# First gate block: four of the eight mixes of the normed rows made by GpSimd in place of VectorE

## The chip, the cores and the metric

The kernel runs on one core of a Trainium2 chip. The metric is the device time of one execution in microseconds (us); lower is better. The kernel before has a median of 2643.79 us over three runs (2643.77 to 2644.37).

## The reference

One layer of an encoder trunk over 512 rows of width 2048, in float32. With h the RMS-normed input:

```python
proj = jnp.einsum('bsd,de->bse', h, w_in[l])
(u_pool, c_b, c_c, c_x, q, k, v, qi, ki, wi, gate_logits) = jnp.split(proj, pts, axis=-1)
...
g = jax.nn.sigmoid(gate_logits).reshape(B, S, N_BRANCH, D)
merged = (g[:, :, 0] * (a @ w_pool_out) + g[:, :, 1] * (bconv @ w_conv_out) + g[:, :, 2] * (c @ w_attn_out))
x = x + merged @ w_o
x = x + square(relu(rmsnorm(x) @ w_ff1)) @ w_ff2
```

The change lies in the product of h with the gate columns of `w_in` (3 x 2048 columns), in the first of its six blocks of 1024 columns.

## The kernel before

**Arithmetic.** TensorE multiplies in a short format, so each operand is split into a rounded part ("hi", a copy by ScalarE) and a rest ("lo", source minus hi, by VectorE), and each product is made of three matmuls: hi with hi, hi with lo, lo with hi. The large products (gates, output projection, MLP) go further: each block of the product is made by a scheme of seven block products in place of eight (numbers n = 0 to 6). For that, quarters of both operands are first added to and subtracted from each other. These sums are the "mixes".

**A gate block** J (0 to 5) is 28 pieces: one for each of the seven products n and each of four groups g of weight rows. The lists `order_of(J)` set the order. For block 0 the order is: (0,g) and (5,g) in turn for g = 0 to 3 (pieces 0 to 7), (1,g) (8 to 11), (4,g) (12 to 15), (3,g) and (2,g) in turn (16 to 23), (6,g) (24 to 27). For each piece ScalarE copies the weight block to `g_wh` (`hi2`, L1473), VectorE makes `g_wl` (`lo2`, L2161), and TensorE runs twelve 128x512 matmuls (L1182 to L1184, function `granule`). The weights have four slots, so the copy of piece k waits until TensorE is done with piece k - 4. The weight blocks land over SyncE's DMA queue.

**The rows' side in block 0.** The normed rows come back from DRAM into `xin` (`h_block`), in two halves h. Products 1, 4, 2 and 3 need mixed quarters. For each (n, h) there are three steps: the mix in `xin` (`mix_gs`), the rounded copy by ScalarE (`hi_gs`, L1598, into `gs` or `act_hi`), and the rest by VectorE (`lo_gs`, L2332, into `gs` or `act_lo`). Their order is

```python
GS_SPLITS = ((1, 0), (1, 1), (4, 0), (4, 1), (2, 0), (3, 0), (2, 1), (3, 1))
```

The semaphores `gs_mixed`, `gs_hi` and `gs_lo` count the three steps. Mix (2,h) overwrites the quarter that mix (1,h) made, so it waits for the rest of (1,h). Mix (3,h) overwrites what mix (2,h) made and waits for the rest of (2,h).

**Where the steps stand.** VectorE's program is a list: after the `lo2` of piece idx, `GS_AFTER[idx]` names the rests and mixes that follow. So the four mixes of products 2 and 3 stand between the splits of pieces 10 to 14. The mixes are L2322 for n = 2 and L2326 for n = 3. ScalarE's program puts `hi_gs` behind the `hi2` of pieces 5, 7, 9, 10, 11, 12, 13 and 14, and the first two copies of gate results (`copy_gate`, L1533) behind pieces 14 and 15. TensorE needs these rests of products 2 and 3 only from piece 16 on, and that of (4,1) at piece 14.

**GpSimd** does no arithmetic on tiles before the change. It issues DMAs that add weight blocks in DRAM (`t_dram`, L2884 to L2893), in a loop that waits for `lo_ready`, `sum_copied`, `sum_paired` and `sum_stored`.

Of the kernel before, what the change touches and what calls it, by code (L numbers as in the profile page):

```python
# [31 lines left out]
ALU = mybir.AluOpType  # L32
# [32 lines left out]
def build(nc, xT, x, cst_dram, w_in, pool_w, w_po, w_co, w_ao, w_o, w_f1, w_f2, out):  # L65
# [31 lines left out]
    with ctx:  # L97
# [128 lines left out]
        def sem(name):  # L226
            return ctx.enter_context(nc.semaphore(name))
# [28 lines left out]
        gs_mixed, gs_hi, gs_lo = sem("gs_mixed"), sem("gs_hi"), sem("gs_lo")  # L256
# [50 lines left out]
        def order_of(J):  # L307
            return FIRST_G if J == 0 else FIRST_W if J == 6 else LAST if J == 15 else NORMAL
# [69 lines left out]
        def gs_at(n, h):  # L378
            return GS_SPLITS.index((n, h)) + 1

        def gs_mix_at(n, h):
            return GS_MIXES.index((n, h)) + 1
# [13 lines left out]
        def h_block(kk, u, h):  # L396
            return xin[:, 8 * kk + 4 * h:8 * kk + 4 * h + 4, 2 * u * P:(2 * u + 2) * P]
# [1493 lines left out]
        def _(dve):  # L1891
# [158 lines left out]
            def mask(t):  # L2050


                i = t + 1
                n = P * (i + 1)
                dst = maskM[:, prob_at[i]:prob_at[i] + n]
                kth = top8[t][:, 7:8]
                above, equal, rank = dst, work[t][:], prob[:, 0:n]
                chain.step(dve.tensor_scalar(above, score[t][:], kth, None, ALU.is_gt, ALU.add,
                                             accum_out=need[:, t:t + 1]))
                chain.step(dve.tensor_scalar(equal, score[t][:], kth, None, ALU.is_equal))  # L2060
                chain.wait()
                chain.step(dve.tensor_scalar(need[:, t:t + 1], need[:, t:t + 1], -1.0, float(TOPK), ALU.mult, ALU.add))
                chain.step(dve.tensor_tensor_scan(rank, equal, equal, 0.0, ALU.add, ALU.max))
                chain.wait()
                chain.step(dve.scalar_tensor_tensor(rank, rank, need[:, t:t + 1], equal, ALU.is_le, ALU.mult))
                chain.wait()
                chain.step(dve.tensor_tensor(dst, dst, rank, ALU.add))
                chain.wait()
                return dve.tensor_scalar(dst, dst, -1.0, -MASKED, ALU.add, ALU.mult)
# [18 lines left out]
            for n in range(4 * UP):  # L2088
# [8 lines left out]
                if n in (0, 2, 4):  # L2097
                    ins = mask(n // 2)
# [92 lines left out]
            for n in range(6 * UP + 1):  # L2191
                h, s = n // 6, n % 6
# [70 lines left out]
                if s == 2:  # L2263
# [4 lines left out]
                    for i in range(TT):  # L2268
                        c = prob_at[i]
                        ins = dve.tensor_scalar(prob[:, c:c + P * (i + 1)], prob[:, c:c + P * (i + 1)],  # L2270
                                                rinv[:, i:i + 1], None, ALU.mult)
# [37 lines left out]
            def mix_gs(n, h):  # L2309

                a11, a12, a21, a22 = h_block(0, 0, h), h_block(1, 0, h), h_block(0, 1, h), h_block(1, 1, h)
                if n == 1:
                    dve.wait_ge(h_back[h][1], 32)
                    ins = dve.tensor_tensor(a22, a21, a22, ALU.subtract)
                elif n == 4:
                    dve.wait_ge(h_back[h][0], 32)
                    dve.wait_ge(gs_mixed, gs_mix_at(1, h))
                    ins = dve.tensor_tensor(a21, a11, a21, ALU.subtract)
                elif n == 2:
                    dve.wait_ge(gs_mixed, gs_mix_at(1, h))  # L2320
                    dve.wait_ge(gs_lo, gs_at(1, h))
                    ins = dve.tensor_tensor(a22, a22, a11, ALU.subtract)  # L2322
                else:
                    dve.wait_ge(gs_mixed, gs_mix_at(2, h))
                    dve.wait_ge(gs_lo, gs_at(2, h))
                    ins = dve.tensor_tensor(a22, a12, a22, ALU.add)  # L2326
                ins.then_inc(gs_mixed, 1)

            def lo_gs(n, h):
# [3 lines left out]
                                  ALU.subtract).then_inc(gs_lo, 1)  # L2333

            GS_AFTER = {3: ((), ((1, 0),)), 5: (((1, 0),), ()), 6: ((), ((1, 1),)), 7: (((1, 1),), ()), 8: ((), ((4, 0),)),
                        9: (((4, 0),), ((4, 1),)), 10: (((4, 1),), ((2, 0),)), 11: (((2, 0),), ((3, 0),)),
                        12: (((3, 0),), ((2, 1),)), 13: (((2, 1),), ((3, 1),)), 14: (((3, 1),), ())}
            for idx, (n, g) in enumerate(order_of(0)):
                if idx > 1:
                    lo2(0, n, g)  # L2340
                splits, mixes = GS_AFTER.get(idx, ((), ()))
                for part in splits:
                    lo_gs(*part)
                for part in mixes:
                    mix_gs(*part)
                if idx == 19:
                    add_gate(0, 0)
                if idx == 26:
                    mix_t1(1, 0)
# [396 lines left out]
            for q in range(1, F1_PAIRS):  # L2746
                for k in range(14):
                    n, h = k // 2, k % 2
# [107 lines left out]
        def _(pool):  # L2856
# [15 lines left out]
            for n in range(14 + 3):  # L2872
# [19 lines left out]
                if n >= 3:  # L2892
                    pool.dma_start(sum_rows_of(n - 3, 3), sum_rows_of(n - 3, 1),  # L2893
                                   max_dma_last_dim=8 * S, accum_op=ALU.add).then_inc(sum_stored, 16)

def constants(norm1, norm2, pool_scale, conv_w, q_gain, k_gain):
# [32 lines left out]
```

## Time and profile before

| what | value |
|---|---|
| median of three runs | 2643.79 us (2643.77 to 2644.37) |
| the profiled execution | 2645.12 us |
| its span, first to last instruction | 2643.3 us |
| TensorE's mean granted clock | 0.999 |
| TensorE busy | 2623.1 us, 99% of the span |
| VectorE busy | 1949.0 us, 74% |
| ScalarE busy | 1241.7 us, 47% |
| GpSimd busy | 94.5 us, 4% |
| instructions | 36093 |

All durations and instants below are of the profiled execution, counted from the start of its span. PE is TensorE, DVE is VectorE, ACT is ScalarE, POOL is GpSimd. A row with "[0.77 <-DVE g_wl L2161]" says that the engine sat idle for 0.77 us just before and that this instruction of VectorE ended the wait. Instructions of one engine overlap a little: a duration of 1.22 us on VectorE goes with a distance of 1.14 us from start to start.

### The profile page before, as it was taken

Reading aid. Unit: us, or ns where it says so; the run is one execution under the profiler, and the core shown is the slowest. Engines: PE = TensorE matmul, PEld = TensorE weight load, DVE = VectorE, ACT = ScalarE, POOL = GpSimd, SP = SyncE. Lnnn points to the kernel's source line nnn. Section 1 sums busy time; section 2 is a strip of 40 time slices with the busy share of each in tenths; the row PEclk is TensorE's granted clock in tenths of the full one; section 3 lists DMA queues with packets and bytes.
Section 4 is the critical chain, followed back from the end, with each engine's and each line's share of the span. In section 5 each row is a group of like instructions: output and inputs, shape, how many; then the busy total and the mean of one; then the engine's idle time right before and its main releaser. Section 6 shows DMA issues by size and latency. Waiting matters only on the chain.

```text
span 2643.3 us, 36093 instructions
## 1 busy us (share of the span) xinstructions
PE 2623.1 (99%) x14114; PEld 2255.0 (85%) x14114; DVE 1949.0 (74%) x2293; ACT 1241.7 (47%) x1615; POOL 94.5 (4%) x116
## 2 busy tenths in 40 slices
PE   8999999999999999999999999999999999999999
PEld 6688877777888888888889999999999788888887
DVE  4565654567777775477569888888887988888887
ACT  6322344335444543234566665656655433333333
POOL 0022222100000000000000000000000000000000
PEclk9999999999999999999999999999999999999999
DMA  7589999956445557556775566566568777685753
GB/s 242 174 230 247 252 254 255 275 175 236 161 160 175 175 175 271 165 169 219 251 231 174 174 211 209 166 218 198 171 219 326 256 273 251 215 318 182 273 188 121
DMA packets 317973, 570.76 MB, mean 216 GB/s; under 512 B 20137, under 2 KB 128297, under 8 KB 317297
## 3 DMA queue, kind: packets, MB, share of 16 engines
q1 hardware_dynamic: 272688, 433.64, 49.4%
q0 software_dynamic: 20736, 58.73, 9.9%
q10 hardware_dynamic: 24384, 76.18, 7.8%
q8 instruction: 107, 1.75, 0.3%
q14 instruction: 58, 0.47, 0.1%
HBM read 476.05 MB, written 151.01 MB: 237 GB/s over the span
## 4 chain that ended last, share of the span: by engine, by line
PE 91%; DVE 4%; DMA 3%; issue 1%; ACT 1%; SPq 0%; ACTq 0%; DVEq 0%
PE aux L1182 8%; PE aux L1184 8%; PE aux L1183 8%; PE main L1286 7%; PE main L1288 7%; PE main L1287 7%; PE main L1182 6%; PE main L1184 6%; PE main L1183 6%; PE main L511 5%; PE main L513 5%; PE main L512 5%; PE main L1217 1%; PE aux L1217 1%; PE aux L1218 1%; PE aux L1219 1%
## 5 line engine op out<-in xcount | busy, mean ns | idle before, releaser
L1286 PE MATMUL main<-sf,f_wh 128*128 128x256 f32 x1728 | 489.3, 283 | 1.1 <-ACT keeps L1773 0.9
L1287 PE MATMUL main<-sf,f_wh 128*128 128x256 f32 x1728 | 489.0, 283 | 0.0
L1288 PE MATMUL main<-sf,f_wl 128*128 128x256 f32 x1728 | 489.0, 283 | 0.0
L1286 PEld LDWEIGHTS main<-sf,f_wh 128*128 128x128 f32 x1728 | 331.7, 192 | 1.8 <-ACT keeps L1773 1.3
L1288 PEld LDWEIGHTS main<-sf,f_wl 128*128 128x128 f32 x1728 | 331.7, 192 | 0.0
L1287 PEld LDWEIGHTS main<-sf,f_wh 128*128 128x128 f32 x1728 | 331.7, 192 | 0.0
L486 DVE TENSOR_TENSOR w_lo<-w_raw,w_hi 128x512 fp32r<-128x512 f32 (+1 forms) x184 | 123.2, 674 | 207.6 <-ACT w_hi L479 206.5
L479 ACT ACTIVATE w_hi<-w_raw 128x512 fp32r<-128x512 f32 (+1 forms) x184 | 113.1, 617 | 269.3 <-PE main L513 209.0
L511 PE MATMUL main<-act_hi,w_hi 128*128 128x512 f32 x576 | 229.9, 399 | 8.0 <-DVE w_lo L486 7.9
L1473 ACT ACTIVATE f_wh<-group 128x1024 fp32r<-128x1024 f32 x128 | 135.7, 1061 | 204.9 <-PE aux L1184 104.1
L513 PE MATMUL main<-act_hi,w_lo 128*128 128x512 f32 x576 | 225.2, 391 | 0.0
L512 PE MATMUL main<-act_lo,w_hi 128*128 128x512 f32 x576 | 225.0, 391 | 0.0
L2617 DVE TENSOR_TENSOR f_wl<-f1raw,f_wh 128x1024 fp32r<-128x1024 f32 x130 | 158.6, 1221 | 65.6 <-ACT f_wh L1754 65.4
L2161 DVE TENSOR_TENSOR f_wl<-group,f_wh 128x1024 fp32r<-128x1024 f32 x128 | 156.4, 1222 | 64.5 <-ACT f_wh L1473 64.3
L1182 PE MATMUL aux<-f_wh,sf 128*128 128x512 f32 x512 | 199.9, 391 | 2.8 <-DVE yb L2773 2.8
L1183 PE MATMUL aux<-f_wl,sf 128*128 128x512 f32 x512 | 199.7, 390 | 0.0
L1184 PE MATMUL aux<-f_wh,sf 128*128 128x512 f32 x512 | 199.7, 390 | 0.0
L1754 ACT ACTIVATE f_wh<-f1raw 128x1024 fp32r<-128x1024 f32 x130 | 136.8, 1055 | 86.1 <-PE main L1288 79.8
L1473 ACT ACTIVATE f_wh<-f2x 128x1024 fp32r<-128x1024 f32 x96 | 102.0, 1063 | 151.3 <-PE aux L1184 83.1
L2161 DVE TENSOR_TENSOR g_wl<-group_g,g_wh 128x1024 fp32r<-128x1024 f32 x80 | 98.0, 1225 | 72.7 <-ACT g_wh L1473 72.7
L1182 PE MATMUL main<-f_wh,sf 128*128 128x512 f32 x384 | 149.6, 390 | 0.8 <-DVE f_wl L2161 0.6
L1183 PE MATMUL main<-f_wl,sf 128*128 128x512 f32 x384 | 149.4, 389 | 0.0
(311 smaller groups left out, 5887.0 us busy)
## 6 DMA issues: line engine op xcount, KB each, us to landing
group<-w_ff SPq DMA_DIRECT2D x160, 512.0 KB, 5.2
f1raw<-w_ff SPq DMA_DIRECT2D x126, 512.0 KB, 5.7
sf<-f_dram ACTq DMA_DIRECT2D x56, 1024.0 KB, 11.7
group_g<-w_in SPq DMA_DIRECT2D x100, 512.0 KB, 4.6
w_raw<-w_in SPq DMA_DIRECT2D x87, 512.0 KB, 8.2
f_dram<-piece_hi SPq DMA_DIRECT2D x112, 256.0 KB, 4.0
f_dram<-piece_lo SPq DMA_DIRECT2D x112, 256.0 KB, 5.1
t_dram<-w_o POOLq DMA_DIRECT2D x48, 512.0 KB, 8.2
```

The source lines that it names most:

```text
L511: pe.matmul(out, wh, hi[:, kt, :], start=(kt == last_kt[0]), stop=False)
L512: pe.matmul(out, wh, lo[:, kt, :], start=False, stop=False)
L513: mm = pe.matmul(out, wl, hi[:, kt, :], start=False, stop=(kt == last_kt[1]))
L1182: pe.matmul(part, sh, wh, start=first, stop=False, skip_group_check=True)
L1183: pe.matmul(part, sh, wl, start=False, stop=False, skip_group_check=True)
L1184: mm = pe.matmul(part, sl, wh, start=False, stop=last, skip_group_check=True)
L1286: pe.matmul(part, hi_at(8, k)[:, cols], sh, start=first, stop=False, skip_group_check=True)
L1287: pe.matmul(part, hi_at(8, k)[:, cols], sl, start=False, stop=False, skip_group_check=True)
L1288: mm = pe.matmul(part, lo_at(8, k)[:, cols], sh, start=False, stop=last, skip_group_check=True)
L1473: act.activation(hi_at(J, k_of(J, n, g))[:], source_of(J, n, g).rearrange("p k c -> p (k c)"), ACT.Copy).then_inc(f_hi, 1)
L2161: dve.tensor_tensor(lo_at(J, k)[:], source_of(J, n, g).rearrange("p k c -> p (k c)"), hi_at(J, k)[:].bitcast(F32), ALU.subtract).then_inc( ...
L2617: dve.tensor_tensor(lo_at(8, k)[:], f1_source(q, n, h).rearrange("p k c -> p (k c)"), hi_at(8, k)[:].bitcast(F32), ALU.subtract).then_inc( ...
```

## The change

VectorE no longer makes the mixes (2,0), (3,0), (2,1) and (3,1). GpSimd makes them, behind its loop of DMA issues, with the same operands and waits of its own. The table `GS_AFTER` loses the four entries. Everything else in VectorE's list keeps its place.

```diff
@@ mix_gs of VectorE
-                elif n == 4:
+                else:
                     dve.wait_ge(h_back[h][0], 32)
                     dve.wait_ge(gs_mixed, gs_mix_at(1, h))
                     ins = dve.tensor_tensor(a21, a11, a21, ALU.subtract)
-                elif n == 2:
-                    dve.wait_ge(gs_mixed, gs_mix_at(1, h))
-                    dve.wait_ge(gs_lo, gs_at(1, h))
-                    ins = dve.tensor_tensor(a22, a22, a11, ALU.subtract)
-                else:
-                    dve.wait_ge(gs_mixed, gs_mix_at(2, h))
-                    dve.wait_ge(gs_lo, gs_at(2, h))
-                    ins = dve.tensor_tensor(a22, a12, a22, ALU.add)
                 ins.then_inc(gs_mixed, 1)
@@ GS_AFTER
-                        9: (((4, 0),), ((4, 1),)), 10: (((4, 1),), ((2, 0),)), 11: (((2, 0),), ((3, 0),)),
-                        12: (((3, 0),), ((2, 1),)), 13: (((2, 1),), ((3, 1),)), 14: (((3, 1),), ())}
+                        9: (((4, 0),), ((4, 1),)), 10: (((4, 1),), ()), 11: (((2, 0),), ()),
+                        12: (((3, 0),), ()), 13: (((2, 1),), ()), 14: (((3, 1),), ())}
@@ GpSimd, behind its loop
+            def mix_gs(n, h):
+
+                a11, a12, a22 = h_block(0, 0, h), h_block(1, 0, h), h_block(1, 1, h)
+                if n == 2:
+                    pool.wait_ge(gs_mixed, gs_mix_at(2, h) - 1)
+                    pool.wait_ge(gs_lo, gs_at(1, h))
+                    ins = pool.tensor_tensor(a22, a22, a11, ALU.subtract)
+                else:
+                    pool.wait_ge(gs_mixed, gs_mix_at(2, h))
+                    pool.wait_ge(gs_lo, gs_at(2, h))
+                    ins = pool.tensor_tensor(a22, a12, a22, ALU.add)
+                ins.then_inc(gs_mixed, 1)
+
+            for n, h in ((2, 0), (3, 0), (2, 1), (3, 1)):
+                mix_gs(n, h)
```

VectorE's list before, from the mix (4,1) to the split of piece 14 (`g_wl` rows are splits of weight pieces, `gs` and `act_lo` rows are rests of the rows' side, `xin` rows are mixes):

```order
563 L2318 TENSOR_TENSOR xin<-xin 128x4x256 [waits gs_mixed,h_back1_0]
564 L2161 TENSOR_TENSOR g_wl_92<-block_g_103,g_wh_88 128x1024 [waits f_hi]
565 L2332 TENSOR_TENSOR act_lo<-xin,act_hi 128x4x256 [waits gs_hi]
566 L2322 TENSOR_TENSOR xin<-xin 128x4x256 [waits gs_lo,gs_mixed]
567 L2161 TENSOR_TENSOR g_wl_93<-block_g_104,g_wh_89 128x1024 [waits f_hi]
568 L2332 TENSOR_TENSOR gs_74<-xin,gs_74 128x1024 [waits gs_hi]
569 L2326 TENSOR_TENSOR xin<-xin 128x4x256 [waits gs_lo,gs_mixed]
570 L2161 TENSOR_TENSOR g_wl_94<-block_g_99,g_wh_90 128x1024 [waits f_hi]
571 L2332 TENSOR_TENSOR gs_75<-xin,gs_75 128x1024 [waits gs_hi]
572 L2322 TENSOR_TENSOR xin<-xin 128x4x256 [waits gs_lo,gs_mixed]
573 L2161 TENSOR_TENSOR g_wl_95<-block_g_100,g_wh_91 128x1024 [waits f_hi]
```

The same place of VectorE's list now:

```order
563 L2318 TENSOR_TENSOR xin<-xin 128x4x256 [waits gs_mixed,h_back1_0]
564 L2161 TENSOR_TENSOR g_wl_92<-block_g_103,g_wh_88 128x1024 [waits f_hi]
565 L2324 TENSOR_TENSOR act_lo<-xin,act_hi 128x4x256 [waits gs_hi]
566 L2161 TENSOR_TENSOR g_wl_93<-block_g_104,g_wh_89 128x1024 [waits f_hi]
567 L2324 TENSOR_TENSOR gs_74<-xin,gs_74 128x1024 [waits gs_hi]
568 L2161 TENSOR_TENSOR g_wl_94<-block_g_99,g_wh_90 128x1024 [waits f_hi]
569 L2324 TENSOR_TENSOR gs_75<-xin,gs_75 128x1024 [waits gs_hi]
570 L2161 TENSOR_TENSOR g_wl_95<-block_g_100,g_wh_91 128x1024 [waits f_hi]
```

The `xin` rows are gone and VectorE's list is two kinds of splits in turn. (Rests are L2324 now.)

The end of GpSimd's list now, from its last DMA issues on:

```order
74 L2882 DMA t_dram<-t_dram 128x1024 [waits sum_stored,sum_paired,sum_copied]
75 L2885 DMA t_dram<-t_dram 128x1024
76 L2885 DMA t_dram<-t_dram 128x1024 [waits sum_stored,sum_paired,sum_copied]
77 L2894 ISA
78 L2894 TENSOR_TENSOR xin<-xin 128x4x256 [waits gs_lo,gs_mixed]
79 L2898 TENSOR_TENSOR xin<-xin 128x4x256 [waits gs_lo,gs_mixed]
80 L2894 TENSOR_TENSOR xin<-xin 128x4x256 [waits gs_lo,gs_mixed]
81 L2898 TENSOR_TENSOR xin<-xin 128x4x256 [waits gs_lo,gs_mixed]
```

The four mixes stand behind all DMA issues. The row ISA is new too and stands in no line of the diff: the built program names it a reload of GpSimd's library. It has no wait of its own.

## Rows read from the trace of the kernel before

**Rows 1.** The page, part 1: busy time of each engine, share of the span

```profile
PE 2623.1 (99%) x14114; PEld 2255.0 (85%) x14114; DVE 1949.0 (74%) x2293; ACT 1241.7 (47%) x1615; POOL 94.5 (4%) x116
```

**Rows 2.** Windows: stretch, length, busy us (instructions), granted clock, DMA share, GB/s

```profile
core 0: us, PE busy (x) PEld busy (x) DVE busy (x) ACT busy (x) POOL busy (x), PEclk, DMA share, GB/s
596.75:599.47 2.72, 2.72 (x14) 2.25 (x13) 2.72 (x4) 2.13 (x2) 0.00 (x0) 1.00 1.03 413
602.20:621.70 19.50, 17.59 (x73) 13.12 (x72) 18.02 (x16) 12.78 (x14) 0.00 (x0) 1.00 0.53 166
621.70:638.02 16.32, 16.32 (x73) 13.52 (x72) 9.72 (x9) 6.37 (x6) 0.00 (x0) 1.00 0.69 221
```

**Rows 3.** Timeline of TensorE: first matmuls of pieces 11, 12, 14, 15 and 16

```profile
604.92 0.50 PE L1182 MATMUL aux<-g_wh,gs 128*128 128x512 f32 x1
608.70 0.47 PE L1182 MATMUL main<-g_wh,act_hi 128*128 128x512 f32 x1 [0.77 <-DVE g_wl L2161]
...
615.87 0.47 PE L1182 MATMUL main<-g_wh,act_hi 128*128 128x512 f32 x1 [0.76 <-DVE g_wl L2161]
...
618.85 0.50 PE L1182 MATMUL main<-g_wh,act_hi 128*128 128x512 f32 x1
...
621.71 0.39 PE L1182 MATMUL aux<-g_wh,gs 128*128 128x512 f32 x1
```

**Rows 4.** Timeline of VectorE from the split of piece 10 on

```profile
600.16 1.22 DVE L2161 TENSOR_TENSOR g_wl<-block_g,g_wh 128x1024 fp32r<-128x1024 f32 x1
601.37 1.23 DVE L2332 TENSOR_TENSOR act_lo<-xin,act_hi 128x1024 fp32r<-128x1024 f32 x1
602.51 1.22 DVE L2322 TENSOR_TENSOR xin<-xin 128x1024 f32<-128x1024 f32 x1
603.65 1.22 DVE L2161 TENSOR_TENSOR g_wl<-block_g,g_wh 128x1024 fp32r<-128x1024 f32 x1
604.86 1.23 DVE L2332 TENSOR_TENSOR gs<-xin,gs 128x1024 fp32r<-128x1024 f32 x1
606.19 1.23 DVE L2326 TENSOR_TENSOR xin<-xin 128x1024 f32<-128x1024 f32 x1
607.34 1.22 DVE L2161 TENSOR_TENSOR g_wl<-block_g,g_wh 128x1024 fp32r<-128x1024 f32 x1
...
614.50 1.22 DVE L2161 TENSOR_TENSOR g_wl<-block_g,g_wh 128x1024 fp32r<-128x1024 f32 x1
615.71 1.23 DVE L2332 TENSOR_TENSOR gs<-xin,gs 128x1024 fp32r<-128x1024 f32 x1
617.57 1.23 DVE L2161 TENSOR_TENSOR g_wl<-block_g,g_wh 128x1024 fp32r<-128x1024 f32 x1 [0.64 <-ACT g_wh L1473]
```

**Rows 5.** Timeline of ScalarE in the same stretch

```profile
603.77 1.06 ACT L1598 ACTIVATE gs<-xin 128x1024 fp32r<-128x1024 f32 x1 [1.49 <-DVE xin L2322]
604.73 1.04 ACT L1473 ACTIVATE g_wh<-block_g 128x1024 fp32r<-128x1024 f32 x1
607.45 1.06 ACT L1598 ACTIVATE gs<-xin 128x1024 fp32r<-128x1024 f32 x1 [1.67 <-DVE xin L2326]
...
614.62 1.06 ACT L1598 ACTIVATE gs<-xin 128x1024 fp32r<-128x1024 f32 x1 [1.68 <-DVE xin L2326]
615.58 1.01 ACT L1533 ACTIVATE gb<-aux 128x1024 f32<-128x1024 f32 x1
616.49 1.05 ACT L1473 ACTIVATE g_wh<-block_g 128x1024 fp32r<-128x1024 f32 x1
```

**Rows 6.** Waits of TensorE from 650 to the end: us in total, times, longest

```profile
PE aux L1182 <- DVE yb L2773: 2.8, 1, 2.8
PE main L1286 <- ACT keeps L1773: 0.9, 2, 0.5
```

**Rows 7.** Timeline of GpSimd: its last instruction of the program

```profile
540.34 0.87 POOL L2893 DMA_DIRECT2D t_dram<-t_dram  x1 [9.69 <-DMA t_dram<-t_dram]
```

**Rows 8.** Timeline of ScalarE: a load of its tables, later in block 0

```profile
645.65 1.28 ACT L1542 ACT_TABLE_LOAD   x1
```

## The prediction

> **What bounds the kernel now.** I read the page's shares first [rows 1]: TensorE is busy 99% of the span, VectorE 74%, GpSimd 4%. So an edit outside TensorE pays only where TensorE waits, and costs only where it makes TensorE wait. Next, the windows [rows 2]. At full pace a piece takes TensorE 2.72 us (first row), and behind piece 16 six pieces take 16.32 us (third row). Between them, from 602.20 to 621.70, six pieces take 19.50. VectorE is busy in 18.02 us of that, so here VectorE sets the pace. The most that any relief can give back is 19.50 - 16.32 = 3.2 us, 0.12% of the time.
>
> The timelines show where it goes. Pieces 11 and 12 start 3.78 us apart [rows 3], 1.06 over 2.72, and TensorE waits for the split `g_wl`. The reader should see three VectorE steps per piece [rows 4]: 603.65 split of a piece, 604.86 rest, 606.19 mix, 607.34 next split. That is 3.69 us for a piece of 2.72. ScalarE is idle between, waiting for the mix [rows 5]. The clock is 1.00 throughout [rows 2] and plays no part.
>
> **Constants.** All come from rows. VectorE: 1.14 from start to start, 1.22 to the end. ScalarE: 0.96 for a copy from start to start; the rest that waits for it starts 1.09 after its start (603.77 to 604.86). Mix end to ScalarE: 0.04. Split start to TensorE start: 1.36 (607.34 to 608.70) [rows 3, 4, 5].
>
> **What is removed.** Four mixes on VectorE, 4 x 1.14 = 4.56 us of its 18.02. In that stretch they are on the path, but only 3.2 us can come back.
>
> **What is added.** Four mixes on GpSimd. They stand behind its DMA issues, the last of which ends at 541.2 [rows 7], so that queue is empty 59 us before the first mix can go, and nothing waits behind them. The ISA row ahead of them has those 59 us as well: I cost it at nothing.
>
> The price d of one mix there is in no row. Lower end 1.22 us, VectorE's own duration for the same operands [rows 4]. Upper end 3.66, as if two reads and one write each took 1.22 in turn. I take 2.4, the middle, which is also two reads in turn. The Trainium skill ("GPSIMD Engine Reference", "3. Performance versus the Vector engine") gives 4497 ns for an add of 2048 columns; half of it, an estimate of 2.25 us, would lower the sum below by some 0.6 us. No row here shows such an operation.
>
> **The path through the mixes.** The four mixes form a chain: (2,0), ScalarE's copy, VectorE's rest, (3,0), then (2,1), which is ready at once, its copy and rest, (3,1), its copy. Behind the last copy ScalarE still has a gate copy and then the weight copy of piece 15: 614.62 to 616.49, 1.87 us [rows 5]. So piece 15 is late when mix (3,1) is, though piece 15 needs none of these mixes. That is where the time is decided.
>
> **Price of two engines at once.** Every VectorE step in this stretch reads two tiles of SBUF, and so does each moved mix. No row has GpSimd reading tiles beside VectorE. Ends: both run at full speed, or they take turns, each blocked while the other runs.
>
> *Taking turns, GpSimd going only when VectorE has nothing ready.* VectorE is out of work at 603.65. Mix (2,0) runs to 606.05, copy 606.09, rest 607.18, split of piece 12 608.32, mix (3,0) 609.46 to 611.86, mix (2,1) to 614.3. Then VectorE has four steps due, to 618.86; mix (3,1) to 621.26, copy 621.30, weight copy of piece 15 at 623.17, its split 624.25, TensorE at 625.6. Before it was 618.85 [rows 3]: 6.8 later.
>
> *Taking turns, GpSimd going first where both are ready.* Mix (2,0) from 601.30 to 603.70; rest (4,1), split of piece 11, rest (2,0) and split of piece 12 to 608.26; mix (3,0) to 610.7, (2,1) to 613.1; four steps to 617.7; mix (3,1) to 620.1; then as above TensorE at 624.5: 5.6 later.
>
> Of both, 0.14 goes off, since piece 16 came 2.86 behind piece 15 before [rows 3] and would come 2.72 behind. The middle is +6.0. Later on nothing takes it back: from 621.70 TensorE runs without a gap [rows 2], and its largest wait behind 650 is 2.8 us for VectorE's results [rows 6], which shift along.
>
> Between the ends I take turns as the likelier. The moved mix shares its operand tile and its kind with steps that the trace only ever shows one after another, and full speed for both needs room for four tile reads at once, of which no row gives an instance. It is a judgement, and I give it little more than half. In a sentence apart: the Trainium skill ("SBUF — State Buffer", "Who interferes with whom") says that a VectorE instruction with two SBUF inputs contends with a GpSimd instruction that reads SBUF, and that the second to start blocks fully; it speaks against this change, and no row here shows it.
>
> **The sum.** Against the profiled execution: 2645.12 + 6.0 = 2651.1. That execution lies 1.33 above the median of the runs, so against the median: 2643.79 + 6.0 = 2649.8.
>
> **Rivals.**
> *Both at full speed, d near 2.4.* Mix (2,0) 600.34 to 602.74, rest 603.87, mix (3,0) 605.2 to 607.6, (2,1) to 610.1, rest 611.2, (3,1) 612.5 to 614.9, copy 615.0, weight copy of piece 15 616.9, split 618.0, TensorE 619.3: 0.5 later than now, less 0.14. TensorE's gaps before pieces 12 to 14 go, and one of 2.4 us before piece 15 takes their place. Time 2644.2. For it: the spare 59 us and ScalarE's idle time [rows 5, 7]. Against it: nothing in the rows. This rival decides against "slower". It holds for d up to 2.9 (+2.4).
> *Full speed, and GpSimd as quick as VectorE, d = 1.22.* The chain shortens by some 3 us: -2.3, 2641.5. This is all but the whole possible gain.
> *Full speed, but GpSimd slow, d = 3.66.* Above 2.3 each us of d costs 4 (four mixes in a chain): +5.5, 2649.3. It passes 0.2% from 3.6 on.
> *The library reload is not over at 541 but is paid by the first mix.* Its price is in no row; the nearest is ScalarE's 1.28 us table load [rows 8], the lower end is nothing. Each us delays the chain by one: with 1.3 us at full speed 2644.2 + 1.3 = 2645.5. In a sentence apart: the skill ("GPSIMD Engine Reference", "2.1 Instruction dispatch") gives about 6 us for a first call to freshly loaded code; by it this would be 2650.2.
>
> **How the numbers follow.** A measurement can tell about 0.2%, 5.3 us, from no change. Turns 0.57 (2649.8); full speed with d near 2.4 0.27 (2644.2); full speed and quick 0.04 (2641.5); full speed and slow 0.07 (2649.3); reload 0.05 (2645.5 and up). Taking turns passes +5.3 for d from 2.0 (GpSimd last) or 2.3 (GpSimd first) on, some 0.74 of its chance: 0.42. Half of the slow case adds 0.04 and the reload 0.02: slower 0.48. No case gains 5.3, since TensorE has only 3.2 to give back; 0.02 for what I don't see: faster 0.02, same 0.50. The range goes from 2642.6 (full speed, d near 1.9) to 2653.2 (turns, d near 3.0). Outside are the quick case and turns with d above 3. The likeliest case's own range is 2647 to 2653.
>
> **What would show it.** GpSimd's four rows: d, and where they start (near 600.3 for full speed, 601.3 or 603.7 for turns). VectorE's rows beside them: 1.22 still, or stretched or delayed by up to d. TensorE's start of piece 15: 625 (turns), 619.3 (full speed). If VectorE's steps keep 1.14 apart while a mix runs, the forecast is wrong. If (2,0) ends more than 4 us after it starts, the reload or the price is.

## The result and the profile after

| | before | changed |
|---|---|---|
| median | 2642.8 us (2639.81 to 2645.15, 17 runs) | 2648.9 us (2646.39 to 2652.29, 17 runs) |
| ratio to before | | 1.0023, 95% interval 1.0016 to 1.0029 |
| profiled execution, span | 2643.3 us | 2649.2 us |

The change costs 6.1 us. The interval corresponds to 4.2 to 7.7 us. The forecast was 2649.8 us, against a kernel before at 2643.79 us: +6.0.

The page of the changed kernel, part 1, beside [rows 1]:

```profile
PE 2625.1 (99%) x14114; PEld 2256.5 (85%) x14114; DVE 1947.3 (74%) x2289; ACT 1244.1 (47%) x1615; POOL 106.8 (4%) x120
```

VectorE has four instructions fewer. At 1.22 us each they would leave 4.9 us less busy time; it is 1.7 us less. GpSimd has 12.3 us more for four mixes, 3.1 each. So the rows of both engines hold time in which one is held up by the other; the timelines below show where.

Windows of the changed kernel, from the end of piece 10 to the start of piece 16 and six pieces further; columns as in [rows 2]:

```profile
602.20:627.13 24.93, 20.13 (x75) 15.45 (x74) 16.93 (x13) 13.24 (x14) 10.75 (x4) 0.86 0.42 136
627.13:643.45 16.32, 16.32 (x73) 13.52 (x72) 9.70 (x9) 6.38 (x6) 0.00 (x0) 1.00 0.68 226
```

The stretch grew from 19.5 to 24.9 us, with TensorE idle for 4.8 of it. Behind it TensorE is again without a gap. VectorE is no longer full: it shows nothing for 8.0 us of the stretch, where it was 1.5. The clock of the stretch is 0.86, where it was 1.00; of piece 13 alone it is 0.50:

```profile
615.56:620.85 5.29, 5.29 (x13) 4.14 (x14) 2.21 (x2) 0.81 (x1) 3.23 (x1) 0.50 0.61 198
```

Timeline of GpSimd in the changed kernel:

```profile
600.78 3.31 POOL L2894 TENSOR_TENSOR xin<-xin 128x1024 f32<-128x1024 f32 x1 [62.01 <-DVE xin L2318]
607.59 3.24 POOL L2898 TENSOR_TENSOR xin<-xin 128x1024 f32<-128x1024 f32 x1 [3.49 <-DVE gs L2324]
610.91 2.38 POOL L2894 TENSOR_TENSOR xin<-xin 128x1024 f32<-128x1024 f32 x1
616.78 3.23 POOL L2898 TENSOR_TENSOR xin<-xin 128x1024 f32<-128x1024 f32 x1 [3.49 <-DVE gs L2324]
```

Timeline of VectorE in the changed kernel, to be read against [rows 4]:

```profile
599.48 1.22 DVE L2318 TENSOR_TENSOR xin<-xin 128x1024 f32<-128x1024 f32 x1
600.61 1.22 DVE L2161 TENSOR_TENSOR g_wl<-block_g,g_wh 128x1024 fp32r<-128x1024 f32 x1
601.83 3.34 DVE L2324 TENSOR_TENSOR act_lo<-xin,act_hi 128x1024 fp32r<-128x1024 f32 x1
605.09 1.21 DVE L2161 TENSOR_TENSOR g_wl<-block_g,g_wh 128x1024 fp32r<-128x1024 f32 x1
606.23 1.21 DVE L2324 TENSOR_TENSOR gs<-xin,gs 128x1024 fp32r<-128x1024 f32 x1
607.37 1.21 DVE L2161 TENSOR_TENSOR g_wl<-block_g,g_wh 128x1024 fp32r<-128x1024 f32 x1
611.96 2.42 DVE L2324 TENSOR_TENSOR gs<-xin,gs 128x1024 fp32r<-128x1024 f32 x1 [3.38 <-ACT gs L1598]
...
623.00 1.23 DVE L2161 TENSOR_TENSOR g_wl<-block_g,g_wh 128x1024 fp32r<-128x1024 f32 x1 [0.64 <-ACT g_wh L1473]
```

Read the two together. Mix (2,0) shows 3.31 us, from 600.78 to 604.09. VectorE's split runs until 601.83, so the mix has some 2.3 us to itself behind it. VectorE's next step is shown from 601.83 with 3.34 us; it ends 1.08 us behind the mix, so it moved data only after it. The third mix starts while VectorE is idle and takes 2.38. VectorE's 2.42 at 611.96 is the tail of that mix, 1.3 us, and then its own 1.1. In all, two steps of VectorE were held up for 3.3 us and three mixes for 2.8. That is little of each engine's time, but it lies in the chain that leads to piece 15.

TensorE in the changed kernel: first matmuls of pieces 11, 13 (with its second), 14, 15 and 16, beside [rows 3]:

```profile
606.36 0.50 PE L1182 MATMUL aux<-g_wh,gs 128*128 128x512 f32 x1 [0.87 <-DVE g_wl L2161]
...
615.56 0.80 PE L1182 MATMUL main<-g_wh,act_hi 128*128 128x512 f32 x1 [3.46 <-DVE g_wl L2161]
616.15 0.63 PE L1183 MATMUL main<-g_wl,act_hi 128*128 128x512 f32 x1
...
620.85 0.45 PE L1182 MATMUL main<-g_wh,act_hi 128*128 128x512 f32 x1
...
624.27 0.50 PE L1182 MATMUL main<-g_wh,act_hi 128*128 128x512 f32 x1 [0.47 <-DVE g_wl L2161]
...
627.13 0.39 PE L1182 MATMUL aux<-g_wh,gs 128*128 128x512 f32 x1
```

**A measure for the experiments.** Whole times scatter by some 5 to 6 us from run to run. So beside the medians I use one distance inside the profile: from VectorE's start of mix (4,1), the last step that the change leaves alone, to TensorE's start of piece 16. Before: 599.02 to 621.71, 22.69 us; [rows 3] has the end, and the start is the row ahead of [rows 4]:

```profile
599.02 1.22 DVE L2318 TENSOR_TENSOR xin<-xin 128x1024 f32<-128x1024 f32 x1
```

Changed: 599.48 to 627.13, 27.65 us, so +4.96. Of the 5.9 us between the spans, 0.46 lies ahead of the stretch, 4.96 in it and 0.48 behind it. The two outer parts are within what single executions differ by. Every distance below is from one profiled execution of its kernel.

### The profile page after: what moved, and what is told of

The parts are those of the page before. It is cut to its first block, busy times and chain, and to the rows that moved or that the text cites. A ratio compares the mean times of both kernels' runs of the same rounds, so it can differ in the third digit from the quotient of the medians.

```text
span 2649.2 us, 36095 instructions
## 1 busy us (share of the span) xinstructions
PE 2625.1 (99%) x14114; PEld 2256.5 (85%) x14114; DVE 1947.3 (74%) x2289; ACT 1244.1 (47%) x1615; POOL 106.8 (4%) x120
## 4 chain that ended last, share of the span: by engine, by line
PE 92%; DVE 4%; DMA 2%; ACT 1%; issue 1%; SPq 0%; POOLq 0%; POOL 0%; ACTq 0%; DVEq 0%
PE aux L1182 8%; PE aux L1183 8%; PE aux L1184 8%; PE main L1286 7%; PE main L1288 7%; PE main L1287 7%; PE main L1182 6%; PE main L1184 6%; PE main L1183 6%; PE main L511 5%; PE main L513 5%; PE main L512 5%; PE main L1028 1%; PE main L1217 1%; PE aux L1217 1%; PE main L1030 1%
## 5 line engine op out<-in xcount | busy, mean ns | idle before, releaser
L1182 PE MATMUL main<-f_wh,sf 128*128 128x512 f32 x384 | 149.6, 390 | 2.4 <-DVE yb L2767 1.3
L1184 PE MATMUL main<-f_wh,sf 128*128 128x512 f32 x384 | 149.4, 389 | 0.0
```

The costliest lines, as they stand in the source:

```text
L1182: pe.matmul(part, sh, wh, start=first, stop=False, skip_group_check=True)
L1184: mm = pe.matmul(part, sl, wh, start=False, stop=last, skip_group_check=True)
```

## Experiments

Two theories at first. **Turns**: the four mixes cost because GpSimd and VectorE take turns at reading two tiles of SBUF. **Detour**: the mixes are slow on GpSimd (2.3 us and the way there and back), and four of them lie in a chain; the blocking is a side show. The experiments also ask whether any work of GpSimd blocks VectorE.

### The chain without reading (e1_chain_only, e5_chain_short)

```diff
-                    ins = pool.tensor_tensor(a22, a22, a11, ALU.subtract)
+                    pool.memset(scr[:, :, :], 0.0).then_inc(masks_ready, 1)
...
+                pool.wait_ge(masks_ready, 1 + gs_mix_at(n, h) - 4)
+                pool.sem_inc(gs_mixed, 1)
```

Both branches of `mix_gs` are changed so; the four mixes are left out, and nothing reads the scratch tile. The clearing covers 128x3072. VectorE waits for the clearings only at block 1.

> The four mixes are left out; in their place GpSimd clears a scratch tile (128x3072, written only, nothing read) behind the same waits and then counts gs_mixed up. The chain through GpSimd stays, with an operation of some 2.6 us (an estimate, the trace shows none). Theory of turns (two operands read from SBUF on both engines are what blocks): VectorE's steps beside it stay 1.22 us long, TensorE starts piece 15 about 1 us later than before, the time is 0 to 2 us over the kernel before. Rival (GpSimd's detour is slow by itself, the blocking is a side show): 4 to 6 us over, as the change. Rival (anything that runs on GpSimd blocks VectorE): VectorE's steps stretched, 5 us or more over.

2647.07 us against 2643.35: ratio 1.0018 (1.0009 to 1.0027), +3.7 us. The distance is 26.01 us, +3.3. That lies between the two expectations on time, so the step lengths have to decide. VectorE's steps beside the clearing keep 1.22 us:

```profile
601.34 2.67 POOL L2896 MEMSET scr<- 128x3072 f32 x1 [58.50 <-DVE xin L2320]
...
602.36 1.23 DVE L2326 TENSOR_TENSOR act_lo<-xin,act_hi 128x1024 fp32r<-128x1024 f32 x1
603.50 1.22 DVE L2162 TENSOR_TENSOR g_wl<-block_g,g_wh 128x1024 fp32r<-128x1024 f32 x1
```

So the clearing, which only writes, does not block. But the detour cost more than expected. Piece 15 started 1.74 us later than before, not about 1 (21.57 us from mix (4,1), against 19.83). The clearing is 0.3 us longer than a mix, four times in a chain, so this run charges the detour with more than the change does; the expectation had all but 0.07 of that, and the rest of the difference is not traced. And piece 15, behind a gap of 2.82 us, ran partly at half clock, 4.44 us in place of 2.72:

```profile
621.59 0.69 PE L1183 MATMUL main<-g_wh,act_hi 128*128 128x512 f32 x1 [2.82 <-DVE g_wl L2162]
```

The second run cuts the scratch tile to `scr[:, 0:5, :]`.

> As the run with the chain only, the cleared scratch tile cut from 3072 to 2560 columns, so that GpSimd's part takes some 2.25 us (2.67 x 2560/3072), as long as a mix runs there once VectorE lets it. The four mixes are left out. By the trace's own constants the detour without blocking costs 0 to 0.5 us. Counted from VectorE's start of mix (4,1) to TensorE's start of piece 16, 22.69 us in the kernel before and 27.65 in the change, theory of turns expects 22.7 to 23.5. If the detour were what costs, 26 or more. In the first such run TensorE ran piece 15 at half clock behind a gap of 2.8 us; with a shorter gap that should not happen.

2644.97 us against 2643.14: ratio 1.0004 (0.9995 to 1.0013), not to be told from before. A clearing takes 2.25 us. The distance is 24.23 us, +1.54. Here I missed the clock: I expected none, and piece 15, behind a gap of only 2.21 us, again took 4.35 us in place of 2.72, 1.63 too much. The window over that piece, granted clock third from the end:

```profile
618.00:622.40 4.40, 4.37 (x13) 3.44 (x14) 3.50 (x3) 2.48 (x3) 0.00 (x0) 0.63 0.65 185
```

Without that the detour costs nothing (1.54 - 1.63). So with nearly the length of an unblocked mix (2.25 against 2.34 us), the detour accounts for 1.5 us at most of the 5.0, all of it clock. The rest needs the blocking.

### Reading and writing beside VectorE (e2_beside_read, e3_beside_write)

The kernel before, all mixes on VectorE; GpSimd does work beside it that nobody uses. In e3 `pool.memset(scr[:, :, :], 0.0)` stands in place of the `tensor_tensor`.

```diff
+            for n, h in ((2, 0), (3, 0), (2, 1), (3, 1)):
...
+                pool.tensor_tensor(scr[:, 0:4, 0:256], act_hi[:, 8:12, 0:256].bitcast(F32), act_hi[:, 8:12, 256:512].bitcast(F32), ALU.add).then_inc(masks_ready, 1)
```

> VectorE keeps all eight mixes as in the kernel before. GpSimd adds four tensor_tensor of the same shape (two reads of SBUF, one write to scratch) at about the same instants, and nothing in the stretch waits for them. Theory of turns: each takes 2.3 to 2.4 us of VectorE's time in the stretch, of which VectorE has none to spare: 6 to 9 us over the kernel before. Rival (the detour of the mixes is slow by itself): no more than 1 us over.

> As the run before, but what GpSimd adds are four clearings of a 128x3072 scratch tile, written only. Theory of turns, by the shared read: VectorE's steps stay 1.22 us and the time is within 1 us of the kernel before. Rival (any GpSimd operation blocks VectorE): some 8 us over.

Reading: 2652.87 us, ratio 1.0037 (1.0023 to 1.0051), +9.5 us; distance 32.46, +9.8. Writing only: 2643.34 us, ratio 1.0001 (0.9992 to 1.001), no difference; distance 22.68, the same as before to 0.01 us. This is the clearest pair: as many GpSimd instructions at about the same instants, and only those that read cost anything. They differ in the operation too, and no run has GpSimd reading one operand alone. With reading, VectorE's steps show it:

```profile
608.66 3.42 POOL L2907 TENSOR_TENSOR scr<-act_hi 128x1024 f32<-128x1024 f32 x1 [4.70 <-DVE gs L2334]
612.25 3.15 POOL L2907 TENSOR_TENSOR scr<-act_hi 128x1024 f32<-128x1024 f32 x1 [0.17 <-POOL scr L2907]
...
608.63 1.23 DVE L2328 TENSOR_TENSOR xin<-xin 128x1024 f32<-128x1024 f32 x1
609.77 3.39 DVE L2162 TENSOR_TENSOR g_wl<-block_g,g_wh 128x1024 fp32r<-128x1024 f32 x1
613.09 3.39 DVE L2334 TENSOR_TENSOR gs<-xin,gs 128x1024 fp32r<-128x1024 f32 x1
```

GpSimd's step waits for the one of VectorE that runs, then runs itself, and VectorE's next waits for it. Each waits about one step of the other. The split that is held up here shares no tile with GpSimd's step, so a shared tile is not the reason. Nothing waited for these four instructions before block 1, so the cost is blocking and what follows from it. Part of that is clock: behind a gap of 2.94 us pieces 14 and 15 took 7.06 us in place of 5.44. Without these 1.6 us the distance is 8.2 us over the kernel before; the 9.5 by the medians lies just above the 6 to 9 that were expected.

### What is held up, and what not (e6_long_read)

The kernel before, with eleven such steps in a row, `pool.wait_ge(g_done, k_of(0, 4, 3) + 1)` ahead of them.

> The kernel before, with eleven tensor_tensor of GpSimd (two reads of SBUF, 128x1024) one behind the other from the end of piece 15 on, where VectorE has time to spare; nothing waits for them before block 1. It shows which of VectorE's steps are held up. Theory of turns by the shared read: the splits (two tiles of SBUF) are stretched by up to the length of a GpSimd step, the one step that reads one tile of SBUF and one of PSUM (gate sum, near 624 us) keeps 1.21 us; the whole within 4 us of the kernel before, since VectorE is half idle there. Rival (any VectorE step is held up): the gate sum is stretched too.

The time, 2653.55 us or +10.4, missed the expectation. My own edit caused it: VectorE's first sum of block 1 waits for the scratch tile, and it waited 7.2 us for GpSimd's eleventh step, which came later than I had reckoned because each of them was held up too. TensorE stood still for 6.6 us behind that. So this total says nothing of the change. The rows do:

```profile
624.66 3.27 POOL L2903 TENSOR_TENSOR scr<-act_hi 128x1024 f32<-128x1024 f32 x1
```

```profile
625.59 1.21 DVE L2300 TENSOR_TENSOR gb<-gb,main 128x1024 f32<-128x1024 f32 x1
626.72 2.29 DVE L2162 TENSOR_TENSOR g_wl<-block_g,g_wh 128x1024 fp32r<-128x1024 f32 x1
```

The gate sum reads one tile of SBUF and one bank of PSUM. It runs wholly inside GpSimd's step and keeps 1.21 us: GpSimd's step, 2.34 us when alone, ends at 627.93 and so moved data from 625.59 on. This is the only step of its kind beside a reading GpSimd. The split behind it reads two tiles of SBUF and ends 1.1 us behind GpSimd's step. Over ten splits the median is 3.41 us, and GpSimd's fastest step, with VectorE idle, took 2.34:

```profile
L2162 DVE TENSOR_TENSOR g_wl<-block_g,g_wh x10: 1219/3408/3426, 620.0 to 645.7; 128x1024 fp32r<-128x1024 f32 x10
```

```profile
L2903 POOL TENSOR_TENSOR scr<-act_hi x11: 2337/3260/3271, 621.4 to 653.8; 128x1024 f32<-128x1024 f32 x11
```

### What there was to win, and how (e4_no_mix, e7_spread_dve, e8_spread_gpsimd)

In e4 GpSimd's `tensor_tensor` gives way to `pool.sem_inc(gs_mixed, 1)`: the kernel leaves the four mixes out.

> The four mixes are left out on both engines; GpSimd only counts gs_mixed up behind the same waits. This measures what VectorE's time in the stretch is worth at most: TensorE's gaps of 3.2 us go, so 3 us under the kernel before. If it is less, the change had nothing to win even with a free GpSimd; if more, the lateness reaches further than the stretch.

2640.77 us against 2643.35: ratio 0.9987 (0.9978 to 0.9996), -2.6 us; distance 19.48, -3.2; TensorE shows no wait between 590 and 640. This bounds what any relief of VectorE here can bring.

e7 relieves VectorE by order alone. The same later places, with the mixes on GpSimd, are e8.

```diff
-                        9: (((4, 0),), ((4, 1),)), 10: (((4, 1),), ((2, 0),)), 11: (((2, 0),), ((3, 0),)),
-                        12: (((3, 0),), ((2, 1),)), 13: (((2, 1),), ((3, 1),)), 14: (((3, 1),), ())}
+                        9: (((4, 0),), ((4, 1),)), 10: (((4, 1),), ()), 11: ((), ((2, 0),)), 12: (((2, 0),), ()),
+                        13: ((), ((3, 0),)), 14: (((3, 0),), ()), 15: ((), ((2, 1),)), 16: (((2, 1),), ()),
+                        17: ((), ((3, 1),)), 18: (((3, 1),), ())}
...
-                    if J == 0 and idx in (5, 7, 9, 10, 11, 12, 13, 14):
+                    if J == 0 and idx in (5, 7, 9, 10, 12, 14, 16, 18):
```

> No GpSimd arithmetic. VectorE keeps all eight mixes, but the last four and their rests are put one to a piece, behind pieces 11 to 18 in place of 10 to 14, and ScalarE's copies of them behind the weight copies of pieces 12, 14, 16 and 18. TensorE needs the rests of products 2 and 3 only from piece 16 on. VectorE's load per piece falls from 3.69 to about 2.3 us, under TensorE's 2.72, so the gaps of 3.2 us go: 2.5 to 3.2 us under the kernel before. If a rest comes too late instead, TensorE waits at pieces 16 to 21 and the time is that of the kernel before or more.

> The change (GpSimd makes the last four mixes) with the same later places for rests and copies as the run before. Theory of turns: two pieces then ask of VectorE three steps of 1.14 and one blocked time of 2.3, 5.7 us against TensorE's 5.44, so a small part of the gaps stays or none: 1 to 3 us under the kernel before, and over the version without GpSimd by 0 to 2 us. The rival (the detour through GpSimd costs by itself) expects the same, since the detour has time here; VectorE's stretched steps would still be seen.

e7: 2639.25 us against 2643.14, ratio 0.9985 (0.9976 to 0.9994), -3.9 us; distance 19.70, -3.0. It beats both kernels and takes what e4 showed to be there; the 2.5 to 3.2 us expected hold by the distance, and the medians give more. e8: 2642.29 us, ratio 0.9999 (0.999 to 1.0008), no difference from before; distance 21.02, -1.7. Against VectorE's own mixes in the same places, GpSimd's cost 1.3 us by the distance (3.0 by the medians), even where the order leaves them time. Both expectations, 1 to 3 us under before and 0 to 2 over e7, hold by the distance and are not shown by the medians.

### Two of four, and the last one later (e9_half, e10_last_later)

```diff
-            for n, h in ((2, 0), (3, 0), (2, 1), (3, 1)):
+            for n, h in ((2, 1), (3, 1)):
```

Mixes (2,0) and (3,0) are back in VectorE's list, where they were before.

> Only mixes (2,1) and (3,1) are GpSimd's, (2,0) and (3,0) stay VectorE's as in the kernel before. Counted from VectorE's start of mix (4,1) to TensorE's start of piece 16 (22.69 us before, 27.65 in the change), theory of turns with a mix of 2.34 us gives 25.9, some 3 us over the kernel before, or more if a gap of over 2 us brings TensorE's clock down where a piece is needed at once. Without blocking the same order would give 22.8.

2647.58 us against 2643.40: ratio 1.0016 (1.0007 to 1.0025), +4.2 us. Distance 28.09, more than in the change with four. In this execution the clock makes the difference. Behind a gap of 2.97 us the whole of piece 15 ran at half clock, 5.29 us:

```profile
622.29 0.80 PE L1182 MATMUL main<-g_wh,act_hi 128*128 128x512 f32 x1 [2.97 <-DVE g_wl L2161]
...
627.58 0.63 PE L1182 MATMUL aux<-g_wh,gs 128*128 128x512 f32 x1
```

Less the 2.57 us over full pace the distance is 25.5; turns expected 25.9, no blocking 22.8. The profiled execution was the slowest of the eleven (2651.64 us), and by the medians, whose intervals overlap, this kernel costs less than the change (4.2 against 6.1), so the fall need not be the rule for it.

For e10 the rest and the copy of (3,1) move behind piece 16 (`16: (((3, 1),), ())`, and 16 in place of 14 in ScalarE's list).

> The change, with ScalarE's copy and VectorE's rest of (3,1) put behind piece 16 in place of piece 14, so that piece 15 no longer waits for the last mix. If that wait is what costs and nothing else, piece 15 starts right behind piece 14, at full clock 24.4 us from mix (4,1) to piece 16, some 2 us over the kernel before. In the change, piece 13 ran at half clock, 5.3 in place of 2.7 us, behind a gap of 3.5 us, hidden under the wait for piece 15; if that repeats, it comes into view here, and only 0.7 us are won: 26.9 us, some 5 over the kernel before.

2646.89 us against 2643.40: ratio 1.0013 (1.0004 to 1.0022), +3.5 us. Distance 26.02, between the two numbers. Piece 15 starts 2.72 us behind piece 14, so its wait for the last mix is gone. Piece 13 still followed a gap of 3.47 us, and eight of its matmuls ran at half clock, 1.7 us in all; with them off, the distance is 24.3, as expected for full clock.

## Why the prediction was right

**Where the time is decided.** Right. VectorE was full in the stretch [rows 2], TensorE waited for its splits [rows 3], and e4 and e7 gave back 3.2 and 3.0 us by the distance, against 3.2 worked out.

**Price of a mix.** 2.4 us taken, 2.34 and 2.38 measured where VectorE was out of the way. The figure of the Trainium skill ("GPSIMD Engine Reference", "3. Performance versus the Vector engine") led to an estimate of 2.25, a little low.

**Turns.** Right, and now shown: a VectorE step that reads two tiles of SBUF and a GpSimd step that reads two exclude each other for their whole length (e2 and e6, 3.4 us in place of 1.2); a clearing, which writes alone, does not block (e3, e1: 1.22 us beside it), and the one step with an operand in PSUM was not blocked (e6, 1.21 us). The Trainium skill ("SBUF — State Buffer", "Who interferes with whom") states just these three cases; the trace agrees with all three.

**Who goes first.** The forecast averaged two orders, which part at mix (2,0): does it go ahead of the rest of (4,1) or behind it and a split? It went ahead, from about 601.75. But VectorE did not yet have that rest ready, since ScalarE's copy for it ended at 601.80:

```profile
600.73 1.07 ACT L1598 ACTIVATE act_hi<-xin 128x1024 fp32r<-128x1024 f32 x1 [0.52 <-DVE xin L2318]
```

At the other three mixes VectorE had nothing ready either, so the change itself never shows the contest. e2 and e6 do: in e2 GpSimd's step waits from 612.25 on, VectorE's next one stands ready, and GpSimd gets in behind the VectorE step that is running. The two alternate.

So the cheaper order came about, with piece 15 at 624.5. It started at 624.27, and 623.8 with the 0.46 us taken off by which this execution was later already at mix (4,1). The mixes' shorter 2.34 us explain part of that.

**The 0.14 us taken off.** Wrong, and small: piece 16 came 2.86 us behind piece 15 as before.

**The clock plays no part.** This step failed. The 1.00 of [rows 2] held for gaps of up to 0.8 us. The change made one of 3.46 us, and piece 13 ran at a granted clock of 0.50, 1.2 in place of 2.4 GHz, for 5.29 us. The time came out right all the same, by luck, because this lay under the wait for piece 15: at full clock piece 14 would have ended near 621.0, and piece 15 could not start before 624.27. In e9 the same fall met piece 15 and was paid in full.

**The rivals.** Both at full speed: out, VectorE's steps are stretched. Quick GpSimd and slow GpSimd: out, by the 2.34. The reload: it is there, long before the mixes, and the first mix is only 0.07 us longer than the second (3.31 and 3.24 us). Nothing of the size of 1.3 us or more shows. The row in the changed kernel, with 0.32 us each:

```profile
L2894 POOLq MODIFY_POOL_CONFIG  x2: 316/316/316, 538.5 to 538.5; - x2
```

**The sum.** +6.0 forecast, +6.1 measured by the medians, +4.96 by the distance. The difference of the last two is not settled: the interval of the medians begins at 4.2. The mechanism was right, but the agreement to 0.1 us is luck. The forecast is the mean of two orders, 6.8 and 5.6 later at piece 15, of which only the second came about, and with the 0.46 taken off piece 15 came 4.96 later.

## What to carry to other kernels

An idle GpSimd was no relief for a VectorE full of steps with two operands in SBUF: a step moved there can hold VectorE up for its own 2.3 us, in place of the 1.14 it saves, and is itself held up by the step that VectorE is running. What cost time here is that both waits lay in a chain with ScalarE's weight copy for piece 15 at its end. In these runs GpSimd's work was free beside VectorE only where it wrote without reading, and beside the one step that read PSUM. Before moving work to another engine, look whether it must stand where it stands; here the order alone, one mix or rest to a piece, gave the 3 to 4 us that the change was reaching for.

## What was not expected of the hardware

TensorE's granted clock fell to half behind single gaps of 2.2 to 3.5 us in an otherwise busy stretch, in the change and in e1, e2, e5, e9 and e10. When it fell and how long it stayed there varied: at once and for 5.3 us in the change and in e9, after six matmuls and with 1.7 us of excess in e10, behind a gap as long as the change's (3.47 and 3.46). Behind gaps of 1.12 us (e1), 1.39 (e9) and 1.82 (e2) it stayed at 1.00.

The kernel before shows it as well, far behind the stretch: its 2.8 us wait in [rows 6]. There half pace followed, a matmul every 0.43 us. Behind the same wait in the changed kernel TensorE ran on at full pace:

```profile
2052.99 0.80 PE L1182 MATMUL aux<-f_wh,sf 128*128 128x512 f32 x1 [2.79 <-DVE yb L2773]
2053.58 0.63 PE L1183 MATMUL aux<-f_wl,sf 128*128 128x512 f32 x1
```

```profile
2059.01 0.50 PE L1182 MATMUL aux<-f_wh,sf 128*128 128x512 f32 x1 [2.79 <-DVE yb L2765]
2059.35 0.40 PE L1183 MATMUL aux<-f_wl,sf 128*128 128x512 f32 x1
```

The next 24 matmuls took 6.92 us in the one and 5.58 in the other. So the same gap is followed by a fall in one execution and by none in another, and one profile of each kernel can't tell how often. A gap in front of a piece thus can have a price beyond itself, up to 2.6 us here, which counts only if the next piece is needed at once.
